# A two-block fp32 model in one kernel: the embeddings' projection in rounded parts, and low parts placed elsewhere on VectorE

## The chip, the cores and the metric

The kernel runs on one core of one Trainium2 chip. The metric is the device time in microseconds (us) of one execution, taken as the median of several runs. PE is TensorE, DVE VectorE, ACT ScalarE, POOL GpSimd, SP SyncE.

## What is computed

256 tokens of width 1024 go through a first block of two layers and a second block of two layers. The change touches only the two layers of the first block. One of them, cut to what matters:

```python
for i in range(DEPTH):                                  # DEPTH = 2
    xn = rmsnorm(h, norm_g[i])
    proj = xn @ w_in[i]                                 # hf hq hi nq kv ... hgo hz nz
    o_hg = hgrn2_chunkwise(hq, log_f, k_hg, hi)         # the gated recurrence
    y_hg = rmsnorm(o_hg, hgrn_onorm_g[i]) * sigmoid(hgo) * silu(hz)
    o_nsa = gates[0] * o_cmp + gates[1] * o_slc + gates[2] * o_win    # three attentions
    y_nsa = o_nsa * silu(nz)
    h = h + concatenate([y_hg, y_nsa]) @ w_out[i]
    gate = sigmoid(rmsnorm(h, ple_norm_g[i]) @ w_pg[i]) # w_pg: 1024 x 1024
    h = h + gate * (p[i] @ w_pp[i])                     # p[i]: 256 x 256, w_pp: 256 x 1024
```

Everything is fp32. `p[i]` are the embeddings of layer i, and `p[i] @ w_pp[i]` is their projection.

## The kernel before

**Panels.** All weights come in panels of 1 MB (128 partitions by 2048 columns, fp32), in the fixed order of `panel_plan`. SP loads them (`load_panel`, DMA issued at line 2831) into one of three raw slots (`RAW`, "panels" in the profile). For nearly all of them ACT then makes a high part, rounded to fp32r (`high_part`, line 1393, "panels_high"), and DVE the low part, raw minus high (`low_part`, line 2026, "panels_low"), each again in three slots. A product of two fp32 matrices is then three fp32r matmuls into one PSUM bank: weights low by input high, weights high by input low, weights high by input high (`product3`, lines 479 to 481). Panels named in `AS_THEY_ARE` (the compression weights, the projection "pp", a small one in block two) have no parts; PE multiplies them as plain fp32 (`small_chunk`, line 497), and their raw slot is free only when PE is done with it.

**Order.** The order on PE is written out by hand. ACT and DVE follow lists that PE's code fills while it is built (`agenda`, `todo`); between steps they make the parts of the next panels wherever `split_high` and `split_low` are called, as far as slots are free by then. Each engine works strictly through its own list. PE waits for a panel by counting low parts (`split`, `pe.wait_ge(low_ready, SPLIT_NO[key] + 1)`), and low parts are made in panel order.

**The recurrence.** Its decay matrices are built in eight levels, each in two halves g = 0, 1. For each, PE multiplies key and query blocks (`level`, line 788), then DVE copies the result out (lines 2271, 2278 or 2282) and multiplies query and key by the forget gates (lines 2300 to 2302), which the next level on PE needs. PE runs the levels in pairs between panels: level 5 between the halves of the panels vv0 and vv1, then the sums of squares of the heads, level 6, a small product ("hid", line 850), the first half of gate panel hgo0 (`gate_chunk`, 24 matmuls at lines 479 to 481), level 7, the second half of hgo0, and so on through hgo1, hz0, hz1, nz0, nz1. DVE's steps there are level 5, "gates" (a low part call, then the attention gates, lines 2334 and 2335), level 6, "hidden" (a low part call, then four small instructions from line 2361), level 7, "k_norm".

**The embeddings.** At the start SP loads `p` of both layers into the tile of q_rope; PE transposes both (line 766, banks 3 and 4) after the panels hi of layer 0; ACT copies them to "p_transposed". Late in each layer, after the output panels wo0 to wo3, PE runs pp: 16 products of 128x128 by 128x256, eight for groups 0 and 1, then the sum of squares of the norm (`folded_sum`, lines 588 and 592), then eight for groups 2 and 3. Next come the panels pg0 to pg3 of the gate, whose input is the normed residual: ACT turns the sum into 1/rms (two instructions on rinv), and DVE and ACT in turn make each of the eight 128x256 chunks (`normed`, lines 1989, 1417, 1985). PE's first matmul on pg0 waits for the first chunk, the next products for the next.

Of the kernel before, what the change touches and what calls it, by code (L numbers as in the profile page):

```python
# [8 lines left out]
P = 128  # L9
T = 256  # L10
NT = T // P
D = 1024
ND = D // P
DEPTH = 2
# [98 lines left out]
ODD_PANELS += [(f"{name}{h}", "mix1_w_in_2", c0 + 256 * h, 256) for name, c0 in  # L113
               (("zg", 512), ("zu", 0), ("fv", 2048)) for h in range(2)]
ODD_PANELS += [(f"wo{g}", "mix1_w_out_2", 256 * g, 256) for g in range(4)]
AS_THEY_ARE = ("cmp0", "cmp1", "pp", "ff")
BY_ROWS = ("hi0", "hi1", "zg0", "zg1", "fv0", "fv1", "vv0", "vv1")
NKH = ND // 2

# [44 lines left out]
def build(nc, a, out):  # L164
# [4 lines left out]
    with ExitStack() as ctx:  # L169
# [5 lines left out]
        def sem(name):  # L175
            if name not in sems:
                sems[name] = ctx.enter_context(nc.semaphore(name))
            return sems[name]
# [111 lines left out]
            flevel[n] = FLV[:, at:at + w]  # L290
            at += w
        xt = FK[:, :].rearrange("p (n d) -> p n d", n=NT)
        ptok = QR[:, :].rearrange("p (l d) -> p l d", l=2 * NT)
        PTR = ctx.enter_context(nc.sbuf_tensor("p_transposed", [P, 1024], F32))
        ptr = PTR[:, :].rearrange("p (l k t) -> p l k t", l=DEPTH, k=2)
        vrows = v3(QN, 8)
        FINAL, OUT, TS = UK[:, :], KZ, SS[:, 0:8]

# [19 lines left out]
        def bank(name):  # L318
            return ps[fills[name][0]]
# [47 lines left out]
        rope_ready, k_rope_ready = sem("q_rope_terms_ready"), sem("k_rope_terms_ready")  # L367
        q_turned, k_turned = sem("q_sine_terms_added"), sem("k_sine_terms_added")
        kz_ready = sem("k_padded_ready")
        blocks_ready = sem("cmp_blocks_ready")  # L370
        gate_exp_ready, gates_ready = sem("gate_exp_ready"), sem("gates_ready")
        hid_exp_ready, hidden_ready = sem("cmp_hidden_exp_ready"), sem("cmp_hidden_ready")
# [48 lines left out]
        def _(pe):  # L421
            last_done = [None]

            def begin(name, b):

                k = bank_fills[b]
                bank_fills[b] += 1
                fills[name] = (b, k)
                if k > 0:
                    pe.wait_ge(psum_free[b], k)  # L430
                return ps[b]
# [315 lines left out]
            for l in range(DEPTH):  # L747
# [8 lines left out]
                        two_chunks(f"hq{g}_{l}", 3 + g, (f"hq{g}", l), normed=nidx if g == 0 else None)  # L756
                tokens([f"hi{n}_{l}" for n in range(NT)], 5, [(f"hi{h}", l) for h in range(2)], normed=l == 0)
                if l == 0:

                    pe.wait_ge(const_landed, 16)  # L760
                    pe.wait_ge(p_landed, 16)
                    for m in range(DEPTH):
                        begin(f"p{m}", 3 + m)
                        for k in range(2):
                            for n in range(NT):
                                ins = pe.transpose(ps[3 + m][:, k * T + n * P:k * T + (n + 1) * P],
                                                   ptok[:, m * NT + n, k * P:(k + 1) * P], ident)
                        done(f"p{m}", ins)

                def level(n, g):  # L770

# [263 lines left out]
                for ks in (range(0, 6), range(6, ND)):  # L1035
                    output_rows(3, ks)

                landed(("pp", l))
                for g in range(4):
                    b = (7, 6, 1, 2)[g]  # L1040
                    if g == 2:
                        folded_sum(nidx)
                    begin(f"pp{g}_{l}", b)
                    for j in range(2):
                        ins = small_chunk(ps[b][:, j * T:(j + 1) * T], raw_panel(("pp", l), 2, 1024),
                                          (2 * g + j) * P, ptr[:, l], nk=2)
                    done(f"pp{g}_{l}", ins)
                release(("pp", l))
                first_two([f"pg{g}_{l}" for g in range(2)], (4, 5), [(f"pg{g}", l) for g in range(2)], nidx)
# [319 lines left out]
        def _(act):  # L1369
# [187 lines left out]
            for l in range(DEPTH):  # L1557
# [18 lines left out]
                for n in range(NT):  # L1576
                    copy_out(f"hi{n}_{l}", vh[:, n, :], bank(f"hi{n}_{l}")[:, :])
                    split_after(f"hi{n}_{l}")
                if l == 0:
                    for m in range(DEPTH):  # L1580
                        copy_out(f"p{m}", PTR[:, m * 512:(m + 1) * 512], bank(f"p{m}")[:, :])
                log_exp()
                dest = {"nq0": QN[:, 0:512], "nq1": QN[:, 512:1024], "ct": PCT[:, :], "hgo0": SG[:, 0:512], "hgo1": SG[:, 512:1024],
                        "hz0": HZ[:, 0:512], "hz1": HZ[:, 512:1024], "nz0": NZ[:, 0:512], "nz1": NZ[:, 512:1024]}
# [108 lines left out]

                split_after(f"wo_{l}_0")
                squares(nidx, lambda g: drained(act, f"wo_{l}_{g}"), lambda g: split_after(f"wo_{l}_{max(g, 1)}") if g != 1 else None)

                def pp_out(g):
                    copy_out(f"pp{g}_{l}", PP[:, g * 512:(g + 1) * 512], bank(f"pp{g}_{l}")[:, :])
# [259 lines left out]
        def _(dve):  # L1958
# [281 lines left out]
            for l in range(DEPTH):  # L2240
# [63 lines left out]

                for g in range(2):
                    split_after(f"hq{g}_{l}")
                in_units = parts_out = False
                for place, kind, *arg in agenda[l]:
                    if kind == "level":
# [18 lines left out]
                        if l == 0:  # L2328
                            bf16_tables()
                    elif kind == "gates":  # L2330
                        split_low(place)
                        for n in range(NT):
                            drained(dve, f"vv{n}_{l}")
                        link(V.tensor_scalar(GT[:, :], GT[:, :], 1.0, None, ALU.add))
# [22 lines left out]
                    elif kind == "hidden":  # L2357
# [8 lines left out]
                        V.tensor_copy(HIDV[:, :].rearrange("p (g r c) -> p g r c", g=2, r=4),  # L2366
                                      HID[:, 32:64].rearrange("p (g c) -> p g c", g=2).unsqueeze(2)
                                      .to_broadcast([P, 2, 4, 16])).then_inc(hidden_ready, 1)
                    elif kind == "cmp_kv":
                        full(dve, f"vc_{l}")  # L2370
                        V.tensor_tensor(v3(VCB, 8), const("head16").unsqueeze(2).to_broadcast([P, 8, 64]),
# [81 lines left out]
                        split_low(place)  # L2453

                add_out(f"wo_{l}_", "", 2 * l + 1)
                normed(2 * l + 1, "ple_norm_g", 8 * l)
                if l == DEPTH - 1:
                    V.memset(PB[:, 0:1024], 0.0).then_inc(bd_zeroed, 1)
# [342 lines left out]
        def _(sp):  # L2801
# [42 lines left out]
            for tile, r, n, c0, c1, src in vec_dmas[1::2]:  # L2844
# [1 line left out]
            load_panel(3)  # L2846
            load_panel(4)
            sp.dma_start(CN[:, 2 * P:], a["const_table"][:, 2 * P:]).then_inc(const_landed, 16)
            sp.dma_start(ptok.rearrange("p (l n) d -> p l n d", l=DEPTH),
                         a["p"][:, 0].rearrange("l (n p) d -> p l n d", p=P)).then_inc(p_landed, 16)  # L2850
            sp.dma_start(LM[:, :], a["mask_table"]).then_inc(masks_landed, 16)
            sp.dma_start(BF[0:8, 0:1], a["fox_bf_2"].rearrange("a h -> h a")).then_inc(bias_landed, 16)

# [24 lines left out]
            for n, (key, *_) in enumerate(LOADS):  # L2878
                if n > SLOTS + 1 and (len(key) == 2 or key[0] != "down" and key[2] == 0):
                    load_panel(n)  # L2880
                name, l, *r = key
                if name == "cmp0":
                    if l > 0:
                        b, k = fills[f"vc_{l - 1}"]
                        sp.wait_ge(psum_full[b], k + 1)
                    for c0, kv in ((0, 0), (64, 0), (P, 1)):
                        sp.dma_start(W2[:, c0:c0 + 64], a["cmp_w2"][l, kv]).then_inc(w2_landed, 16)
                if name == "ga1":
                    sp.wait_ge(bd_zeroed, 1)
                    for at, w in ((0, "lru_wa_2"), (512, "lru_wx_2")):  # L2890
                        src = a[w][0].rearrange("(c r) i j -> r i c j", r=2)
                        for r in range(2):
                            dst = PB[64 * r:64 * r + 64, at:at + 512].rearrange("p (c m) -> p c m", c=4)
                            sp.dma_start(dst[:, :, 64 * r:64 * r + 64], src[r]).then_inc(bd_landed, 16)
                if name == "fk0":
                    sp.dma_start(FINAL, a["final_norm_2"].unsqueeze(0).to_broadcast([P, D])).then_inc(gain_landed, 16)
                    sp.dma_start(PT[:, 0:1024].rearrange("p (h s) -> p h s", h=8),
                                 a["sgu_w_2"][0].rearrange("h t s -> t h s")).then_inc(sgu_landed, 16)
                    for h in range(8):
                        r, c = h % 2, h // 2  # L2900
                        sp.dma_start(AC[64 * r:64 * r + 64, c * P:(c + 1) * P],
                                     a["sgu_b_2"][0, h:h + 1, :].to_broadcast([64, P])).then_inc(bt_landed, 16)
                if name == "value" and r == [0]:
                    ffn(l)
# [27 lines left out]
```

## Time and profile before

| What | Value |
|---|---|
| median of 3 runs | 971.55 us (971.46 to 971.69) |
| the profiled execution | 971.99 us, its span 970.0 us |
| PE busy | 953.6 us, 98% of the span, 7618 matmuls |
| DVE busy | 754.3 us, 78% |
| ACT busy | 615.6 us, 63% |
| mean granted TensorE clock | 0.999 of full |
| DMA | 164.33 MB, 169 GB/s |

The profile is of one execution, and its span runs from the first to the last instruction. A matmul's length in the timeline is that of its passage through the array; matmuls overlap, so what one costs is read from the distance between two starts. Plain fp32 products stand in the timeline as two records each. A time in brackets is idle time of that engine just before the row, with what ended it.

### The profile page before, as it was taken

The numbers are of one execution on the slowest core, as the hardware profiler recorded it, in microseconds if no ns is written. First come the engines' busy times: TensorE is split into PE (matmuls) and PEld (weight loads), VectorE is DVE, ScalarE is ACT, GpSimd is POOL, SyncE is SP. The second block draws the span as 40 slices with busy tenths as digits, with TensorE's granted clock in tenths as the row PEclk, the third lists the DMA queues.
The fourth block names the chain that finished last, engine by engine and source line by source line (L and its number), as shares of the span: only waits on it lengthen the run. The fifth ranks groups of instructions, "written<-read, shape, count | busy, mean of one in ns | idle before, by whom it ended". The sixth has DMA issues, their size and how long they took to land.

```text
span 970.0 us, 18775 instructions
## 1 busy us (share of the span) xinstructions
PE 953.6 (98%) x7618; PEld 875.2 (90%) x7618; DVE 754.3 (78%) x1132; ACT 615.6 (63%) x914; POOL 19.7 (2%) x33
## 2 busy tenths in 40 slices
PE   6999999999999999999999999999999999999997
PEld 6998989999989889999999999999998988888886
DVE  7967876797678777998788877778878598777685
ACT  5744885676447856787477556557657566555554
POOL 2000200000002000000000000000000000000000
PEclk9999999999999999999999999999999999999999
DMA  9666422465664233745546656557283446655541
GB/s 304 197 181 219 139 88 87 137 214 183 173 218 139 66 110 115 244 156 188 179 133 215 218 175 200 187 174 222 93 271 110 141 135 219 203 181 176 191 152 44
DMA packets 143869, 164.33 MB, mean 169 GB/s; under 512 B 6686, under 2 KB 130216, under 8 KB 143800
## 3 DMA queue, kind: packets, MB, share of 16 engines
q1 hardware_dynamic: 142408, 161.90, 51.9%
q0 software_dynamic: 928, 0.52, 0.4%
q8 instruction: 51, 0.84, 0.4%
q10 hardware_dynamic: 464, 0.93, 0.3%
q14 instruction: 18, 0.15, 0.0%
HBM read 161.89 MB, written 1.05 MB: 168 GB/s over the span
## 4 chain that ended last, share of the span: by engine, by line
PE 87%; DVE 5%; ACT 4%; DMA 2%; issue 1%; SPq 0%; DVEq 0%; ACTq 0%
PE ps L479 19%; PE ps L480 18%; PE ps L481 18%; PE ps L1259 14%; PE ps L1257 7%; DMA panels<-in_w_in 2%; DVE panels_low L2026 2%; ACT panels_high L1393 2%; PE ps L497 1%; PE ps L692 1%; PE ps L717 1%; PE ps L788 1%; PE ps L1299 1%; DVE squares L1989 1%; PE ps L703 1%
## 5 line engine op out<-in xcount | busy, mean ns | idle before, releaser
L2026 DVE TENSOR_TENSOR panels_low<-panels,panels_high 128x2048 fp32r<-128x2048 f32 (+1 forms) x145 | 327.5, 2261 | 63.2 <-ACT panels_high L1393 62.6
L1393 ACT CAST panels_high<-panels 128x2048 fp32r<-128x2048 f32 (+1 forms) x145 | 273.4, 1887 | 85.7 <-PE ps L481 63.2
L479 PE MATMUL ps<-input_parts,panels_low 128*128 128x256 f32 x832 | 240.2, 289 | 0.2 <-DVE panels_low L2026 0.2
L480 PE MATMUL ps<-input_parts,panels_high 128*128 128x256 f32 x832 | 235.2, 283 | 0.0
L481 PE MATMUL ps<-input_parts,panels_high 128*128 128x256 f32 x832 | 235.1, 283 | 0.0
L1259 PE MATMUL ps<-input_parts,panels_high 128*128 128x512 f32 x608 | 214.0, 396 | 0.0
L1257 PE MATMUL ps<-input_parts,panels_low 128*128 128x256 f32 x608 | 170.6, 281 | 0.7 <-DVE panels_low L2026 0.7
L479 PEld LDWEIGHTS ps<-input_parts,panels_low 128*128 128x128 f32 x832 | 159.2, 191 | 2.4 <-issue 1.7
L480 PEld LDWEIGHTS ps<-input_parts,panels_high 128*128 128x128 f32 x832 | 159.3, 191 | 0.7 <-issue 0.5
L481 PEld LDWEIGHTS ps<-input_parts,panels_high 128*128 128x128 f32 x832 | 159.3, 191 | 0.0
L1259 PEld LDWEIGHTS ps<-input_parts,panels_high 128*128 128x128 f32 x608 | 114.1, 188 | 26.4
L1257 PEld LDWEIGHTS ps<-input_parts,panels_low 128*128 128x128 f32 x608 | 114.7, 189 | 2.5 <-issue 1.3
L479 PE MATMUL ps<-ffn_hidden_high,panels_low 128*128 128x256 f32 x320 | 91.2, 285 | 1.1 <-DVE panels_low L2026 1.0
L481 PE MATMUL ps<-ffn_hidden_high,panels_high 128*128 128x256 f32 x320 | 90.4, 283 | 0.0
L480 PE MATMUL ps<-ffn_hidden_low,panels_high 128*128 128x256 f32 x288 | 81.2, 282 | 0.0
L479 PEld LDWEIGHTS ps<-ffn_hidden_high,panels_low 128*128 128x128 f32 x320 | 60.8, 190 | 2.1 <-DVE panels_low L2026 1.2
L481 PEld LDWEIGHTS ps<-ffn_hidden_high,panels_high 128*128 128x128 f32 x320 | 60.2, 188 | 0.0
L480 PEld LDWEIGHTS ps<-ffn_hidden_low,panels_high 128*128 128x128 f32 x288 | 54.2, 188 | 0.3
L1923 ACT CAST ffn_hidden_high<-values_hg 128x512 fp32r<-128x512 f32 x22 | 13.7, 621 | 57.1 <-DVE values_hg L2707 53.7
L1892 ACT COPY forget_key<-ps 128x512 f32<-128x512 f32 x36 | 21.0, 583 | 44.5 <-PE ps L1259 44.5
L479 PE MATMUL ps<-unscaled,panels_low 128*128 128x256 f32 x160 | 46.2, 289 | 0.0
L481 PE MATMUL ps<-unscaled,panels_high 128*128 128x256 f32 x160 | 45.2, 283 | 0.0
(342 smaller groups left out, 1626.6 us busy)
## 6 DMA issues: line engine op xcount, KB each, us to landing
panels<-in_ffn_up SPq DMA_DIRECT2D x44, 1024.0 KB, 5.0
panels<-in_w_in SPq DMA_DIRECT2D x29, 1024.0 KB, 5.8
panels<-in_ffn_down SPq DMA_DIRECT2D x22, 1024.0 KB, 4.9
panels<-in_mix_w_in SPq DMA_DIRECT2D x20, 1024.0 KB, 5.7
panels<-in_w_out SPq DMA_DIRECT2D x8, 1024.0 KB, 5.3
panels<-in_w_pg SPq DMA_DIRECT2D x8, 1024.0 KB, 5.1
panels<-in_mix_w_out SPq DMA_DIRECT2D x8, 1024.0 KB, 5.2
panels<-in_w_in SPq DMA_DIRECT2D x6, 512.0 KB, 5.7
```

The source lines that it names most:

```text
L479: pe.matmul(dst, w[1], x[0], start=start, stop=False if not kw else True, **kw)
L480: pe.matmul(dst, w[0], x[1], start=False, stop=False if not kw else True, **kw)
L481: return pe.matmul(dst, w[0], x[0], start=False, stop=stop, **kw)
L497: ins = pe.matmul(dst, w3[:, k, col:col + m], x3[:, k, :], start=(k == 0), stop=(k == nk - 1))
L692: ins = pe.matmul(ps[b + r][:, 0:2 * w].rearrange("p (k s) -> p k s", k=2), q[h, n * P:(n + 1) * P], keys[h, :, r, 0:w], start=False, stop ...
L703: pe.transpose(ps[6][:, r * T:r * T + P], probs[bb][0][:, r, :], ident)
L1257: pe.matmul(both[:, 0, :], w_low, xh3[:, k, :], start=(k == 0), stop=True, skip_group_check=True)
L1259: ins = pe.matmul(both, w_high, x_parts[:, :, k, :], start=False, stop=True, skip_group_check=True)
L1393: nc.scalar.copy(high_slots[slot][:, 0:size], raw[n % SLOTS][:, 0:size]).then_inc(high_ready, 1)
L1892: nc.scalar.copy(sums[par][:, s, :], up_halves[half][:, :, 0, :]).then_inc(half_out, 1)
L1923: nc.scalar.copy(gh3[par], hidden[par]).then_inc(gh_ready, 1)
L2026: V.tensor_tensor(low_slots[slot][:, 0:size], raw[n % SLOTS][:, 0:size], high_slots[slot][:, 0:size].bitcast(F32), ALU.subtract).then_inc( ...
```

## The change

The panel pp is no longer taken as it is: it gets a high and a low part like the others, and its products become three fp32r matmuls each (`product3`). With that, each later panel stands one place further in the count of parts and in the three slots. The transposed embeddings get two parts as well: ACT rounds the transposed PSUM bank to a high part, DVE subtracts it for the low part, ahead of recurrence level 0. The tile has room for one layer, so the transposes are made once in each layer, and `p` of layer 1 is loaded after pg0 of layer 0. In the norm after the output panels, ACT and DVE make the parts of one more panel, pg1, after those of pg0 (`split_after(f"wo_{l}_3")`). In DVE's step "gates" the call for low parts is gone; "hidden" keeps its call at its start and gets a second one at its end.

```diff
-AS_THEY_ARE = ("cmp0", "cmp1", "pp", "ff")
+AS_THEY_ARE = ("cmp0", "cmp1", "ff")
...
-        ptok = QR[:, :].rearrange("p (l d) -> p l d", l=2 * NT)
-        PTR = ctx.enter_context(nc.sbuf_tensor("p_transposed", [P, 1024], F32))
-        ptr = PTR[:, :].rearrange("p (l k t) -> p l k t", l=DEPTH, k=2)
+        ptok = v3(QR, 4)[:, 0:NT, :]
+        PTR = ctx.enter_context(nc.sbuf_tensor("p_transposed_parts", [P, 1024], F32R))
+        p_parts = PTR[:, :].rearrange("p (s k t) -> p s k t", s=2, k=2)
...
                 if l == 0:
-
                     pe.wait_ge(const_landed, 16)
-                    pe.wait_ge(p_landed, 16)
-                    for m in range(DEPTH):
-                        begin(f"p{m}", 3 + m)
-                        for k in range(2):
-                            for n in range(NT):
-                                ins = pe.transpose(ps[3 + m][:, k * T + n * P:k * T + (n + 1) * P],
-                                                   ptok[:, m * NT + n, k * P:(k + 1) * P], ident)
-                        done(f"p{m}", ins)
+                pe.wait_ge(p_landed, 16 * (l + 1))
+                begin(f"p{l}", 3)
+                for k in range(2):
+                    for n in range(NT):
+                        ins = pe.transpose(ps[3][:, k * T + n * P:k * T + (n + 1) * P], ptok[:, n, k * P:(k + 1) * P],
+                                           ident)
+                done(f"p{l}", ins)
...
-                landed(("pp", l))
+                split(("pp", l))
+                drained(pe, f"p{l}")
+                w = parts(("pp", l), 2, 1024)
...
-                        ins = small_chunk(ps[b][:, j * T:(j + 1) * T], raw_panel(("pp", l), 2, 1024),
-                                          (2 * g + j) * P, ptr[:, l], nk=2)
+                        c = (2 * g + j) * P
+                        for k in range(2):
+                            ins = product3(ps[b][:, j * T:(j + 1) * T], [t[:, k, c:c + P] for t in w],
+                                           (p_parts[:, 0, k, :], p_parts[:, 1, k, :]), k == 0, k == 1)
...
@@ ACT @@
-                if l == 0:
-                    for m in range(DEPTH):
-                        copy_out(f"p{m}", PTR[:, m * 512:(m + 1) * 512], bank(f"p{m}")[:, :])
+                full(act, f"p{l}")
+                nc.scalar.copy(PTR[:, 0:512], bank(f"p{l}")[:, :]).then_inc(ph_ready, 1)
...
                 squares(nidx, lambda g: drained(act, f"wo_{l}_{g}"), lambda g: split_after(f"wo_{l}_{max(g, 1)}") if g != 1 else None)
+                split_after(f"wo_{l}_3")
...
@@ DVE, ahead of the agenda's levels @@
+                dve.wait_ge(ph_ready, l + 1)
+                V.tensor_tensor(PTR[:, 512:1024], bank(f"p{l}")[:, :], PTR[:, 0:512].bitcast(F32),
+                                ALU.subtract).then_inc(free(f"p{l}"), 1)
...
                     elif kind == "gates":
-                        split_low(place)
                         for n in range(NT):
                             drained(dve, f"vv{n}_{l}")
...
                     elif kind == "hidden":
                         split_low(place, SPLIT_NO[("hgo1", l)] + 1)
...
+                        split_low(place, SPLIT_NO[("hgo1", l)] + 1)
...
                 add_out(f"wo_{l}_", "", 2 * l + 1)
+                split_after(f"wo_{l}_3")
                 normed(2 * l + 1, "ple_norm_g", 8 * l)
...
@@ SP @@
-            sp.dma_start(ptok.rearrange("p (l n) d -> p l n d", l=DEPTH),
-                         a["p"][:, 0].rearrange("l (n p) d -> p l n d", p=P)).then_inc(p_landed, 16)
+            psrc = a["p"][:, 0].rearrange("l (n p) d -> l p n d", p=P)
+            sp.dma_start(ptok, psrc[0]).then_inc(p_landed, 16)
...
+                if (name, l) == ("pg0", 0):
+                    b, k = fills["n0D1_3"]
+                    sp.wait_ge(psum_full[b], k + 1)
+                    sp.dma_start(ptok, psrc[1]).then_inc(p_landed, 16)
```

**Where instructions move.** First place: DVE in each layer of the first block, at the steps "gates", level 6 and "hidden". "panels_low" is the low part of a panel, here of hgo0 and hgo1 (x2); "nsa_gates" is the step "gates"; "decay_diag", "gate_o", "query", "forget_key" are level 6, half 0 then half 1; "small" opens the step "hidden". Before:

```order
L2026 TENSOR_TENSOR panels_low<-panels,panels_high 128x2048 [waits panel_high_ready] x2
L2334 TENSOR_SCALAR nsa_gates<-nsa_gates 128x48 [waits psum_free6,psum_free5]
L2335 RECIPROCAL nsa_gates<-nsa_gates 128x48 [waits vector_step]
L2278 COPY decay_diag<-ps 32x4x32 [waits psum_full7]
...
L2300 TENSOR_TENSOR gate_o<-gate_o 128x8 [waits vector_step,hg_level_ready]
L2301 TENSOR_TENSOR query<-query,gate_o 128x8x32
L2302 TENSOR_TENSOR forget_key<-forget_key,gate_o 128x8x32
L2278 COPY decay_diag<-ps 32x4x32 [waits psum_full0]
...
L2361 TENSOR_SCALAR small<-small 128x64 [waits cmp_hidden_exp_ready]
```

And in the changed kernel:

```order
L2339 TENSOR_SCALAR nsa_gates<-nsa_gates 128x48 [waits psum_free6,psum_free5]
L2340 RECIPROCAL nsa_gates<-nsa_gates 128x48 [waits vector_step]
L2281 COPY decay_diag<-ps 32x4x32 [waits psum_full7]
...
L2303 TENSOR_TENSOR gate_o<-gate_o 128x8 [waits vector_step,hg_level_ready]
L2304 TENSOR_TENSOR query<-query,gate_o 128x8x32
L2305 TENSOR_TENSOR forget_key<-forget_key,gate_o 128x8x32
L2281 COPY decay_diag<-ps 32x4x32 [waits psum_full0]
...
L2029 TENSOR_TENSOR panels_low<-panels,panels_high 128x2048 [waits panel_high_ready] x2
L2366 TENSOR_SCALAR small<-small 128x64 [waits cmp_hidden_exp_ready]
```

Both low parts moved from ahead of the gates and level 6 to behind both halves of level 6.

Second place: PE at the same point, the same in both kernels. The first two rows are level 6 (halves 0 and 1), the third is "hid", the fourth the first matmul on gate panel hgo0:

```order
L788 MATMUL ps<-query,forget_key 32x32 [waits psum_free7,hg_level_ready]
...
L788 MATMUL ps<-query,forget_key 32x32 [waits psum_free0,hg_level_ready]
...
L850 MATMUL ps<-consts,nsa_z 128x32 [waits psum_free3]
...
L479 MATMUL ps<-input_parts,panels_low 128x256 [waits panel_low_ready,psum_free6]
...
L788 MATMUL ps<-query,forget_key 64x64 [waits psum_free7,hg_level_ready]
```

Nothing moved here: the matmul on hgo0 waits for a low part and stands ahead of level 7 (the last row, half 0).

Third place: ACT at the norm after the output panels. "squares" is the square of a quarter of the residual, "rinv" the 1/rms, "panels_high" the high part of a panel. In the changed kernel:

```order
L1396 CAST panels_high<-panels 128x2048 [waits psum_full3,panel_landed1]
L1382 ACTIVATE squares<-residual 128x512 [waits psum_free5]
L1396 CAST panels_high<-panels 128x2048 [waits psum_full5,panel_landed2]
L1382 ACTIVATE rinv<-ps,eps 128x256 [waits psum_full0]
L1382 ACTIVATE rinv<-rinv 128x256 [waits psum_free0]
L1420 CAST input_parts<-squares 128x256 [waits normed_f32_ready] x8
```

The second cast, of pg1, is new here; before, the square is followed by rinv at once. On DVE a second low part stands likewise between the last sum of the residual and the first instruction of `normed`.

## Rows read from the trace of the kernel before

**Rows 1.** The page: busy time, engines of the last chain, cast to high parts.

```profile
PE 953.6 (98%) x7618; PEld 875.2 (90%) x7618; DVE 754.3 (78%) x1132; ACT 615.6 (63%) x914; POOL 19.7 (2%) x33
...
PE 87%; DVE 5%; ACT 4%; DMA 2%; issue 1%; SPq 0%; DVEq 0%; ACTq 0%
...
L1393 ACT CAST panels_high<-panels 128x2048 fp32r<-128x2048 f32 (+1 forms) x145 | 273.4, 1887 | 85.7 <-PE ps L481 63.2
```

**Rows 2.** Waits of PE, whole span: total, times, longest us.

```profile
PE ps L788 <- DVE forget_key L2302: 1.5, 2, 0.8
```

**Rows 3.** Timeline of PE, layer 0: start us, length us, engine, line, operation.

```profile
87.17 0.70 PE L788 MATMUL ps<-query,forget_key 128*32 128x32 f32 x32
...
88.26 0.36 PE L479 MATMUL ps<-input_parts,panels_low 128*128 128x256 f32 x1
...
92.79 0.68 PE L788 MATMUL ps<-query,forget_key 128*64 128x64 f32 x8 [0.80 <-DVE forget_key L2302]
```

**Rows 4.** Timeline of DVE there; in brackets the idle time before, and its releaser.

```profile
84.23 2.29 DVE L2026 TENSOR_TENSOR panels_low<-panels,panels_high 128x2048 fp32r<-128x2048 f32 x1 [1.12 <-ACT panels_high L1393]
87.07 2.29 DVE L2026 TENSOR_TENSOR panels_low<-panels,panels_high 128x2048 fp32r<-128x2048 f32 x1 [0.55 <-ACT panels_high L1393]
...
89.87 0.52 DVE L2278 COPY decay_diag<-ps 32x128 f32<-32x128 f32 x2
...
92.32 0.42 DVE L2302 TENSOR_TENSOR forget_key<-forget_key,gate_o 128x256 f32<-128x256 f32 x1
```

**Rows 5.** Timeline of PE at the embeddings' projection, layer 0.

```profile
177.80 3.62 PE L497 MATMUL ps<-p_transposed,panels 128*128 128x256 f32 x16
181.25 0.59 PE L588 MATMUL ps<-squares,consts 128*128 128x256 f32 x2
...
182.55 3.62 PE L497 MATMUL ps<-p_transposed,panels 128*128 128x256 f32 x16
...
186.12 0.28 PE L480 MATMUL ps<-input_parts,panels_high 128*128 128x256 f32 x1
186.24 0.28 PE L481 MATMUL ps<-input_parts,panels_high 128*128 128x256 f32 x1
```

**Rows 6.** Timeline of ACT and DVE at the norm beside it.

```profile
182.75 0.47 ACT L1379 ACTIVATE rinv<-ps,eps 128x256 f32<-128x256 f32 x1 [3.17 <-PE ps L592]
...
183.71 0.88 DVE L1989 SCALAR_TENSOR_TENSOR squares<-residual,vectors,rinv 128x256 f32<-128x256 f32 x2 [2.45 <-ACT rinv L1379]
184.66 0.43 DVE L1985 TENSOR_TENSOR input_parts<-squares,input_parts 128x256 fp32r<-128x256 f32 x1
```

**Rows 7.** Timeline of ACT and DVE at the first recurrence level.

```profile
49.78 1.08 ACT L1384 COPY p_transposed<-ps 128x512 f32<-128x512 f32 x2
...
49.99 0.69 DVE L2288 TENSOR_TENSOR query<-query,forget_key 128x512 f32<-128x512 f32 x1
...
55.42 0.30 DVE L2271 COPY_PREDICATED decay_blocks<-level_masks,ps 128x128 f32<-128x128 int32 x1 [2.54 <-PE ps L788]
```

**Rows 8.** Windows at the end; the third number from the right is the clock.

```profile
964.00:965.00 1.00, 0.26 (x2) 0.00 (x0) 0.32 (x1) 0.69 (x2) 0.00 (x0) 1.00 0.00 0
...
966.00:967.00 1.00, 0.00 (x0) 0.00 (x0) 1.00 (x2) 0.00 (x0) 0.00 (x0) 1.00 0.59 246
967.00:968.00 1.00, 0.00 (x0) 0.00 (x0) 0.19 (x1) 0.00 (x0) 0.00 (x0) 0.71 0.98 387
968.00:969.00 1.00, 0.00 (x0) 0.00 (x0) 0.00 (x0) 0.00 (x0) 0.00 (x0) 0.50 1.00 385
```

**Rows 9.** Timeline of PE's first microseconds.

```profile
8.96 1.97 PE L611 MATMUL ps<-consts,forget_key 128*128 128x128 f32 x8 [1.15 <-DMA forget_key<-in_x]
...
11.15 0.41 PE L481 MATMUL ps<-ffn_hidden_high,panels_high 128*128 128x256 f32 x1
11.37 0.41 PE L479 MATMUL ps<-ffn_hidden_high,panels_low 128*128 128x256 f32 x1
...
11.75 0.28 PE L481 MATMUL ps<-ffn_hidden_high,panels_high 128*128 128x256 f32 x1
```

More of the change, by code:

```diff
@@ L369, in build @@
         kz_ready = sem("k_padded_ready")
+        ph_ready = sem("p_transposed_high_ready")
         blocks_ready = sem("cmp_blocks_ready")
```

## Prediction

> **What bounds the kernel now.** The page comes first. PE is busy for 98% of the span and holds 87% of the chain that ended last, DVE is at 78% and ACT at 63% [rows 1]. So work that is taken from PE, or a wait put on it, moves the end by about its own length; work on DVE and ACT counts only where PE waits for it. Second, the list of PE's waits. Most belong to the start; of those inside the layers the largest is for the recurrence: 1.5 us, twice, 0.8 us at most [rows 2]. It is level 7, half 1, once in each layer, and layer 1 repeats layer 0 at this place to within 0.1 us. Third, the timelines around the two places that are edited.
>
> A difference of 0.2% (1.9 us) is about what a measurement can tell here from no change. The sum below is a difference, made in the profiled execution of 971.99 us (span 970.0 us, and 2.0 us around it); it is added to the median of 971.55 us, which lies 0.4 us under that execution.
>
> **The low parts moved behind level 6.** Before, DVE makes the low part of hgo0 from 84.23 us and that of hgo1 from 87.07 us, 2.29 us each, and starts level 6 late, at 89.87 us; its last instruction starts at 92.32 us and ends at 92.74 us. Level 7, half 1, starts on PE 0.05 us after that, at 92.79 us, with 0.80 us of idle time ahead [rows 3, 4]. Moving the low parts away frees this chain, which is worth the 1.5 us in the two layers.
>
> But PE wants hgo0 before level 7. Its first matmul on that panel starts at 88.26 us [rows 3], 1.7 us after the low part is there (84.23 + 2.29 = 86.52). In the changed kernel the low part is behind both halves of level 6 in DVE's own list, and DVE cannot pass them. Level 6 is first on PE: it starts at 87.17 us and half 0, half of 0.70 us, is done at 87.52 us [rows 3]. DVE then needs 92.74 - 89.87 = 2.87 us for both halves [rows 4]. So:
> - DVE starts level 6 at 87.52 + 0.05 = 87.57 us and ends it at 90.44 us;
> - the low part of hgo0 takes 2.29 us, to 92.73 us;
> - PE starts on hgo0 at about 92.8 us in place of 88.26 us: 4.5 us later.
>
> What else is queued there: behind PE's wait stands everything, since PE runs in its own order. On DVE the low part of hgo1 ends 2.3 us later, at 95.0 us, which PE wants only a panel half, level 7 and another half after 92.8 us, so not before 99 us. Then "hidden" and level 7 follow, some 2.5 us later than before, while PE itself is 4.5 us later: no second wait. The loads of the panels that reuse these raw slots go out up to 6 us later, for casts that stand behind PE by more than that.
>
> Net in each layer: 4.5 us new wait, less the wait on level 7. For both: 2 x 4.5 - 1.5 = **+7.5 us**. The bounds: were DVE faster by its pipelining (level 6 in 2.4 us, the distance of its first and last start, 92.32 - 89.87) it is 4.0 us each, +6.5; were the hand-overs 0.15 us each instead of 0.05, +7.9.
>
> **The projection in rounded parts.** Before, 32 records of plain fp32 a layer: 16 between 177.80 and 181.25 us, 3.45 us, then the norm's sum, then 16 more from 182.55 us; the matmuls at the fp32r pace go on from 186.12 - 0.12 = 186.00 us, again 3.45 us [rows 5]. Together 6.9 us. After: 48 fp32r matmuls at the distance of 186.24 - 186.12 = 0.12 us [rows 5], 5.76 us. That is 1.15 us less on PE in each layer.
>
> Not all of it arrives, since pg0 waits for the norm. The sum now ends 0.6 us earlier, and ACT, idle for 3.17 us before 182.75 us, could answer at 182.2 us. But DVE has a new low part (pg1) in the 2.45 us that it was idle before 183.71 us [rows 6]: the cast of pg1 can start on ACT at 182.75 - 3.17 = 179.58 us, takes 1.89 us [rows 1], so DVE works on it from 181.5 to 183.8 us. The norm's first instruction on DVE then starts at 183.8 us, where it stood before, 0.1 us later in fact. Its first chunk was ready at 184.66 + 0.43 = 185.09 us [rows 6] and is ready at 185.2 us now, against PE's 184.85 us. So PE resumes at 185.25 us in place of 186.00 us: 0.75 us gained per layer, and I take it that the later chunks come as fast as PE uses them (six matmuls each, 0.72 us). For both layers **-1.5 us**, within -2.3 us (the norm holds nothing up) and -0.6 us (cast or low part of pg1 half a microsecond late). A rule of the Trainium skill speaks for more: "FP8 and Floating Point Precision", section "TensorE Precision Notes", has true fp32 as four passes through the array. By it, three products instead of four passes would save a quarter, 1.7 us a layer instead of 1.15 us; the trace shows 6.9 against 5.76 us and decides.
>
> **The embeddings' parts.** PE makes the same eight transposes, four of them in each layer: nothing in sum. Casts and low parts are added: DVE gets 0.69 us (a 128x512 instruction) ahead of level 0, and must wait for ACT's one copy, which ended at 49.78 + 0.54 = 50.3 us. Level 0's four instructions, which ended at 50.68 us, then end at about 53 us, and the low part of the next panel at 55.3 us. DVE was idle for 2.54 us before level 1 at 55.42 us, so this just fits [rows 7]. I cost it at nothing; if its cover were gone, it would be 0.5 us in a layer. The load of `p` of layer 1 moves 256 KB beside panels of 1 MB; SP's added wait is for scores that PE finishes before wo3 is split, which the next panel load waits for anyway. Nothing.
>
> **The clock.** This is the unknown. PE has no wait of 4.5 us inside the layers now. At the end of the run it stops at 964.26 us; the granted clock is still 1.00 in the window from 966 us, 0.71 in the next, 0.50 (1.2 GHz) from 968 us [rows 8]. It fell about 3.1 us after the last matmul. A wait of 4.5 us is longer than that. At the start, matmuls begin again at 8.96 us, are 0.22 us apart at 11.15 us and of full-speed length from 11.75 us [rows 9]: 2.8 us of slow work, of which 1 - 0.12/0.22, some 1.25 us, are lost. So each wait costs between 0 (the clock holds) and 1.25 us. One instance of a fall does not say that it always comes so soon; I take one fall in two waits, **+1.2 us**, and keep 0 and +2.5.
>
> **Sum.** 7.5 - 1.5 + 1.2 = +7.2 us, so 971.55 + 7.2 = **978.7 us**, slower by 0.7%.
>
> **The rivals.**
> - The clock holds in both waits: 7.5 - 1.5 = +6.0, 977.5 us. For it: one example of a fall, at the end of the run, is thin. Chance 0.28.
> - It falls in both: 7.5 - 1.5 + 2.5 = +8.5, 980.0 us. For it: the wait is longer than the 3.1 us of rows 8 each time. Chance 0.27. The Trainium skill sides with it: "TensorE: Matmul & The Clock Gate", section "HAM oscillation — how this bites in real kernels", says that idle gaps between bursts of matmuls put the engine back to half its clock, and each gap pays anew.
> - **Faster**: the low part of hgo0 does arrive before PE wants it, and only hgo1's stands behind level 6. The high part is there at 84.2 us, where DVE stood idle for it [rows 4], so there is room for 2.29 us before 88.26 us. Then level 7 waits no more (-1.5), the projection gives -1.5 to -2.3: -3.4, 968.1 us. The point that decides is whether the low part ends by 88.26 us. Against it stands the order of the changed kernel, where both low parts follow level 6. Chance 0.04.
> - **No change**: PE's delay is taken up further on, because another engine sets the end after all. It would need waits of PE behind the layers that shrink by 6 us; with PE busy for 98% of the span [rows 1] and no wait over 0.8 us in the layers there is next to nothing to give back. 971.5 us, chance 0.04.
>
> My forecast, one fall in two, has 0.37.
>
> **Range and chances.** 975.8 to 981.2 us: it spans the three clock cases, with 1 to 1.5 us for a new wait of 4.0 instead of 4.5 us and a projection worth 0.6 to 2.3 us. All three are slower by over 0.2%: 0.92. Within 0.2%: 0.04. Faster: 0.04.
>
> **What will show it.** In the changed kernel's trace PE has a wait for "panels_low" of over 4 us in each layer, right behind level 6 and "hid", released by the low part of hgo0; the wait for forget_key at level 7 is gone; DVE is idle ahead of level 6 and has both low parts behind it. Matmuls on p_transposed_parts stand 0.12 us apart, and pg0 starts up to 0.2 us after them with DVE as releaser. In the windows behind the new waits the granted clock is 1.00 or lower, which decides among the three cases. I am wrong if PE goes from "hid" to hgo0 without a gap, or if such a gap is under 3 us.

## The result, and the profile after

The changed kernel takes 982.24 us (median of 4 runs, 981.97 to 982.35) against 971.60 us before (971.46 to 971.69): +10.6 us, a ratio of 1.0108 [1.0096, 1.0120]. The forecast was 978.7 us and its range ended at 981.2 us. The sign and the place were right, the size was not. Two lines of the page of the profiled execution, and its span:

```profile
span 980.3 us, 18849 instructions
PE 956.4 (98%) x7650; PEld 879.5 (90%) x7650; DVE 759.9 (78%) x1136; ACT 618.7 (63%) x916; POOL 19.7 (2%) x33
PE 85%; DVE 6%; ACT 5%; issue 2%; DMA 1%; SPq 0%; DVEq 0%; ACTq 0%
```

Beside [rows 1], PE's share of the chain has fallen by 2 points; DVE, ACT and "issue" have each gained one, and DMA has lost one. PE is still busy for 98% of the span. But its busy time *rose* by 2.8 us, though 2.3 us of matmul work was taken out of the projection. At a lower clock PE is busy for longer with the same work (matmuls 0.21 us apart instead of 0.12, below), so a busy time that rises where work was removed is the first sign of the clock. The list of PE's waits:

```profile
PE ps L480 <- DVE panels_low L2029: 9.9, 5, 4.5
PE ps L604 <- DMA q_nope<-in_norm_g: 6.3, 1, 6.3
PE ps L1260 <- DVE panels_low L2029: 0.8, 2, 0.4
PE ps L480 <- DVE input_parts L1988: 0.5, 2, 0.2
```

The wait for forget_key of [rows 2] is gone. In its place stands one for panels_low: 9.9 us in five waits, the longest 4.5 us. The third row belongs to both kernels, and so does a wait of some 6 us at the start (5.7 us before, 6.3 us here). DVE's timeline in layer 0 shows why:

```profile
87.15 0.58 DVE L2281 COPY decay_diag<-ps 32x128 f32<-32x128 f32 x2 [1.71 <-PE ps L787]
...
89.66 0.42 DVE L2305 TENSOR_TENSOR forget_key<-forget_key,gate_o 128x256 f32<-128x256 f32 x1
90.00 4.49 DVE L2029 TENSOR_TENSOR panels_low<-panels,panels_high 128x2048 fp32r<-128x2048 f32 x2
```

Level 6 starts on DVE at 87.15 us, 2.7 us earlier than in [rows 4], and takes 2.85 us to the start of the two low parts. The 4.49 us are both of them, shown as one row; hgo0's is the first half, done by 92.3 us. PE's timeline there, and the same row in layer 1:

```profile
86.66 0.70 PE L787 MATMUL ps<-query,forget_key 128*32 128x32 f32 x32
87.29 0.63 PE L849 MATMUL ps<-consts,nsa_z 128*128 128x32 f32 x4
92.43 0.55 PE L480 MATMUL ps<-input_parts,panels_low 128*128 128x256 f32 x1 [4.51 <-DVE panels_low L2029]
92.78 0.42 PE L481 MATMUL ps<-input_parts,panels_high 128*128 128x256 f32 x1
92.99 0.42 PE L482 MATMUL ps<-input_parts,panels_high 128*128 128x256 f32 x1
...
97.77 1.14 PE L787 MATMUL ps<-query,forget_key 128*64 128x64 f32 x16
...
293.74 0.55 PE L480 MATMUL ps<-input_parts,panels_low 128*128 128x256 f32 x1 [4.51 <-DVE panels_low L2029]
```

The last row is the one of layer 1. Two things are to be seen. PE is idle for 4.51 us in front of hgo0, once in each layer. And behind it the matmuls are not 0.12 us apart but 0.21 us (92.78 to 92.99): the 24 of this panel half take 5.34 us, from 92.43 to level 7 at 97.77 us. The windows across that place (PEclk is the third number from the right):

```profile
88.00:90.00 2.00, 0.00 (x0) 0.00 (x0) 1.93 (x8) 2.00 (x3) 0.00 (x0) 1.00 0.00 0
90.00:91.00 1.00, 0.00 (x0) 0.00 (x0) 1.00 (x2) 0.97 (x2) 0.00 (x0) 0.91 0.00 0
91.00:97.00 6.00, 4.57 (x21) 4.60 (x22) 4.60 (x6) 2.43 (x4) 0.00 (x0) 0.50 0.61 194
97.00:98.00 1.00, 1.00 (x9) 0.83 (x8) 0.00 (x0) 0.00 (x0) 0.00 (x0) 0.68 1.09 350
...
292.00:293.00 1.00, 0.00 (x0) 0.00 (x0) 1.00 (x1) 1.00 (x3) 0.00 (x0) 0.60 0.00 0
293.00:299.00 6.00, 5.26 (x24) 5.19 (x24) 3.90 (x6) 1.74 (x3) 0.00 (x0) 0.50 0.72 232
299.00:300.00 1.00, 1.00 (x16) 0.89 (x16) 0.17 (x1) 0.00 (x0) 0.00 (x0) 0.98 1.11 350
```

The granted clock falls to its lower level (0.50, 1.2 GHz) within the wait, in both layers, and stays there for nearly the whole panel half. A row that holds both levels gives the moment: 0.91 in the row from 90 us puts the fall at 90.8 us, 0.60 in the one from 292 us at 292.2 us, 2.9 and 3.0 us after PE's last matmul; the rise is at 97.6 and 299.0 us. The Trainium skill, "TensorE: Matmul & The Clock Gate", section "HAM oscillation — how this bites in real kernels", describes this course: each gap between bursts pays for a slow start anew. The trace agrees on that. The section counts 1.67 us of throttled time per gap, in a kernel whose bursts of 16 matmuls are about 2 us long; here the burst goes on, and the rows show 5.3 us of slow work.

Where the time went, from the starts of the same instructions in both traces: PE is 0.5 us ahead of the kernel before at level 6 of layer 0 (four of the eight transposes now stand in layer 1). Past level 7 it is 5.45 us behind, past the projection 4.67, past layer 1's transposes 5.11, past layer 1's level 7 11.19, and past its projection 10.42 us behind, which stays to the end. So the moved low parts cost 6.0 and 6.1 us, the projection gives 0.8 us twice, and the transposes give 0.5 us and take 0.4.

### The profile page after: what moved, and what is told of

Same layout as the page of the kernel before. It is cut to its first block, busy times and chain, and to the rows that moved or that the text cites. A ratio compares the mean times of both kernels' runs of the same rounds, so it can differ in the third digit from the quotient of the medians.

```text
span 980.3 us, 18849 instructions
## 1 busy us (share of the span) xinstructions
PE 956.4 (98%) x7650; PEld 879.5 (90%) x7650; DVE 759.9 (78%) x1136; ACT 618.7 (63%) x916; POOL 19.7 (2%) x33
## 4 chain that ended last, share of the span: by engine, by line
PE 85%; DVE 6%; ACT 5%; issue 2%; DMA 1%; SPq 0%; DVEq 0%; ACTq 0%
PE ps L480 19%; PE ps L481 18%; PE ps L482 18%; PE ps L1262 14%; PE ps L1260 7%; ACT panels_high L1396 2%; DVE panels_low L2029 2%; PE ps L693 1%; PE ps L787 1%; PE ps L718 1%; DMA panels<-in_w_in 1%; PE ps L598 1%; DVE squares L1992 1%; PE ps L1302 1%; DVE input_parts L1988 1%
## 5 line engine op out<-in xcount | busy, mean ns | idle before, releaser
L2029 DVE TENSOR_TENSOR panels_low<-panels,panels_high 128x2048 fp32r<-128x2048 f32 (+1 forms) x147 | 332.0, 2262 | 59.1 <-ACT panels_high L1396 58.5
L1396 ACT CAST panels_high<-panels 128x2048 fp32r<-128x2048 f32 (+1 forms) x147 | 277.1, 1886 | 85.2 <-PE ps L482 63.9
L481 PE MATMUL ps<-input_parts,panels_high 128*128 128x256 f32 x832 | 237.7, 286 | 0.0
L482 PE MATMUL ps<-input_parts,panels_high 128*128 128x256 f32 x832 | 237.6, 286 | 0.0
L481 PEld LDWEIGHTS ps<-input_parts,panels_high 128*128 128x128 f32 x832 | 161.6, 194 | 0.6 <-issue 0.5
L482 PEld LDWEIGHTS ps<-input_parts,panels_high 128*128 128x128 f32 x832 | 161.6, 194 | 0.0
L1262 PEld LDWEIGHTS ps<-input_parts,panels_high 128*128 128x128 f32 x608 | 114.3, 188 | 26.1
```

The source lines that it names most:

```text
L481: pe.matmul(dst, w[0], x[1], start=False, stop=False if not kw else True, **kw)
L482: return pe.matmul(dst, w[0], x[0], start=False, stop=stop, **kw)
L1262: ins = pe.matmul(both, w_high, x_parts[:, :, k, :], start=False, stop=True, skip_group_check=True)
L1396: nc.scalar.copy(high_slots[slot][:, 0:size], raw[n % SLOTS][:, 0:size]).then_inc(high_ready, 1)
L2029: V.tensor_tensor(low_slots[slot][:, 0:size], raw[n % SLOTS][:, 0:size], high_slots[slot][:, 0:size].bitcast(F32), ALU.subtract).then_inc( ...
```

## The experiments

All were compared with the kernel before on the same chip: 971.53 us for the first four, 971.86 us for the last four.

**e1: the low parts back ahead of the gates.** The rest of the change stays.

```diff
                     elif kind == "gates":
+                        split_low(place)
                         for n in range(NT):
```

> The changed kernel with the call for low parts put back at its old place in DVE's step gates, so that both low parts (hgo0, hgo1) stand ahead of level 6 again; everything of the projection stays. Theory (all of the loss comes from the moved low parts and the clock after them): 971.6 - 1.6 = 970.0 us, the 0.8 and 0.7 us waits at level 7 back, no wait of PE over 1 us after the start, granted clock 1.00 throughout the layers. Rival (the projection's added casts, low parts and slots cost the part of the loss that I had not counted, some 3.5 us): 974 to 975 us.

Measured 969.89 us (969.66 to 970.17), ratio 0.9983 [0.9973, 0.9992], mean clock 0.999; level 7 waits for forget_key again (1.4 us in two). The projection and the embeddings' parts without the moved low parts give 1.6 us, as the sum had it (1.5).

**e2: the move alone**, made in the kernel before.

```diff
                     elif kind == "gates":
-                        split_low(place)
                         for n in range(NT):
```

> The kernel before with the call for low parts taken out of the step gates and nothing else changed. Theory: two waits of 4.5 us on the low part of hgo0, each followed by some 5 us at half clock, minus the waits at level 7: 971.6 + 12.0 = 983.6 us, the granted clock 0.50 for about 7 us in each of the two layers. Rival (the projection carries 3.5 us of the loss): 979 to 980 us.

Measured 983.13 us (981.86 to 983.98), ratio 1.0114 [1.0097, 1.0131]. Its waits of PE:

```profile
PE ps L479 <- DVE panels_low L2026: 9.7, 5, 4.5
```

With e1 this places the loss in the call that is gone: 983.13 - 971.53 = +11.6 us for it and -1.6 us for the rest make +10.0 us, beside the +10.6 us of both together; the 0.6 us between them are within the spread of e2's runs (2.1 us).

**e3: PE kept busy through the wait.** 36 more matmuls ahead of the one on hgo0, on data that are there, into a bank that the real products then overwrite; they are no part of the reference's computation.

```diff
                         begin(f"{name}{g}_{l}", b)
+                        if key[0] == "hgo0":
+                            for i in range(36):
+                                pe.matmul(ps[b][:, 0:T], xh3[:, i % ND, 0:P], xh3[:, i % ND, :], start=True,
+                                          stop=True, skip_group_check=True)
                         split(key)
```

> The changed kernel with 36 more fp32r matmuls of 128x256 (4.3 us at 0.12 us apart) on PE ahead of its wait for hgo0; their result is overwritten by the first matmul on hgo0. Theory (the clock falls because PE stands still): the wait is filled, the granted clock stays 1.00, PE resumes when the low part is there, as before, and the work after it is at full speed: 982.2 - 2 x 2.35 = 977.5 us. Rival (the slow stretch behind the wait has another cause, such as DMA traffic or operands that come late): no change, 982.2 us.

Measured 977.23 us (976.99 to 977.70), ratio 1.0058 [1.0042, 1.0075]. The timeline, then windows over the place:

```profile
87.80 4.55 PE L805 MATMUL ps<-input_parts 128*128 128x256 f32 x36
92.38 0.39 PE L480 MATMUL ps<-input_parts,panels_low 128*128 128x256 f32 x1
...
95.45 1.15 PE L787 MATMUL ps<-query,forget_key 128*64 128x64 f32 x16
```

```profile
90.00:92.00 2.00, 2.00 (x19) 2.00 (x18) 2.00 (x2) 1.97 (x5) 0.00 (x0) 1.00 0.00 0
92.00:94.00 2.00, 1.97 (x16) 1.77 (x16) 2.00 (x2) 1.49 (x2) 0.00 (x0) 1.00 0.19 35
94.00:97.00 3.00, 3.00 (x33) 2.80 (x32) 2.47 (x8) 0.00 (x0) 0.00 (x0) 1.00 1.05 360
```

The first real matmul starts at 92.38 us, in the changed kernel at 92.43: the wait is as long, it is only filled. But the panel half now takes 3.07 us (92.38 to 95.45) instead of 5.34, and the kernel is 5.0 us faster for 72 added matmuls. So the clock alone costs 2.27 us at this place and 5.0 us in all (4.7 us between the two profiled spans, 980.3 and 975.6 us), and the delay of the low part makes the rest: 977.23 us is the forecast's case "the clock holds", 977.5 us. DMA traffic as the cause of the slow stretch is ruled out with it: the loads still run (360 GB/s from 94 us), and the clock stays at 1.00.

**e4: only hgo0's low part back ahead of the gates.**

```diff
                     elif kind == "gates":
+                        split_low(place, SPLIT_NO[("hgo0", l)] + 1)
                         for n in range(NT):
```

> The changed kernel with only the low part of hgo0 put back ahead of level 6; that of hgo1 stays behind it. Theory: hgo0 is there 1.7 us before PE wants it, level 6 is done early enough for level 7 (its 1.5 us in two layers go), and hgo1's low part ends near 92.8 us, 4 us before PE wants it: 971.6 - 1.5 - 1.6 = 968.5 us. Rival (level 7 or hgo1 becomes late in its place): 970.0 us or more, with a wait of PE on panels_low or forget_key there.

Measured 967.86 us (967.69 to 968.28), ratio 0.9961 [0.9947, 0.9975]. DVE's timeline:

```profile
82.88 2.28 DVE L2029 TENSOR_TENSOR panels_low<-panels,panels_high 128x2048 fp32r<-128x2048 f32 x1
...
90.34 2.29 DVE L2029 TENSOR_TENSOR panels_low<-panels,panels_high 128x2048 fp32r<-128x2048 f32 x1
```

and PE's waits on the two releasers in question (none is on forget_key):

```profile
PE ps L1260 <- DVE panels_low L2029: 0.7, 2, 0.4
PE ps L480 <- DVE input_parts L1988: 0.5, 2, 0.2
PE ps L480 <- DVE panels_low L2029: 0.4, 2, 0.2
```

One low part ahead of level 6 and one behind it meets both of PE's needs. This is the place and the price of the forecast's "faster" rival (968.1 us), which the change itself did not make.

**e5: the same in the kernel before**, to see whether the parts add up.

```diff
                     elif kind == "gates":
-                        split_low(place)
+                        split_low(place, SPLIT_NO[("hgo0", l)] + 1)
                         for n in range(NT):
```

> The kernel before with hgo0's low part left ahead of level 6 and only hgo1's moved behind it; the projection stays plain fp32. Theory (the two parts of the change add up): the waits at level 7 go, 971.5 - 1.5 = 970.0 us, so that e4 (967.9) is this plus the projection's 1.6 to 2.0 us. Rival (e4's gain needs both parts together, since the projection shifts the panels' slots): no change, 971.5 us.

Measured 969.84 us (969.67 to 970.03), ratio 0.9979 [0.9969, 0.9988]. With e1: -2.0 - 1.6 = -3.6 us, and e4 has -3.7. The two parts add up. The gain of 2.0 us is more than the 1.5 us of level 7's waits: its two halves take 1.07 us of PE's time without the wait (97.77 to 98.84 us in the changed kernel) and took 2.09 us with it (91.31 to 93.40 us in the kernel before), 1.0 us less in each layer.

**e6: half as many matmuls in the wait**, 18 instead of 36, so that PE is idle for 2.2 us.

```diff
-                            for i in range(36):
+                            for i in range(18):
```

> As e3_pe_kept_busy, with 18 matmuls (2.2 us) in place of 36, at the start of the wait, so that PE still stands still for 2.4 us. Theory (the clock falls some 3 us after PE's last matmul, as at 90.9 and 292.6 us in the changed kernel's windows): the clock holds, 977.3 us as with 36. Rival (any wait of 2 us or more in place of work brings it down): between 980 and 982 us, granted clock 0.50 behind the wait.

Measured 979.85 us (978.63 to 980.71), ratio 1.0078 [1.0062, 1.0093]: a miss for the expectation that such a short wait leaves the clock alone. The timeline, then the windows:

```profile
87.82 2.38 PE L805 MATMUL ps<-input_parts 128*128 128x256 f32 x18
92.40 0.58 PE L480 MATMUL ps<-input_parts,panels_low 128*128 128x256 f32 x1 [2.20 <-DVE panels_low L2033]
...
96.92 1.15 PE L787 MATMUL ps<-query,forget_key 128*64 128x64 f32 x16
```

```profile
91.00:92.00 1.00, 0.00 (x0) 0.00 (x0) 1.00 (x1) 1.00 (x3) 0.00 (x0) 1.00 0.00 0
92.00:93.00 1.00, 0.60 (x2) 0.60 (x3) 1.00 (x2) 0.97 (x2) 0.00 (x0) 0.67 0.00 0
93.00:95.00 2.00, 2.00 (x11) 2.00 (x11) 1.97 (x3) 0.53 (x1) 0.00 (x0) 0.50 0.69 191
95.00:96.00 1.00, 1.00 (x8) 1.00 (x7) 0.69 (x3) 0.00 (x0) 0.00 (x0) 0.63 1.09 383
96.00:98.00 2.00, 2.00 (x26) 1.80 (x24) 0.37 (x2) 0.00 (x0) 0.00 (x0) 1.00 1.10 362
...
292.00:293.00 1.00, 0.16 (x1) 0.17 (x2) 1.00 (x2) 0.97 (x3) 0.00 (x0) 1.00 0.00 0
293.00:294.00 1.00, 1.00 (x8) 1.00 (x9) 1.00 (x1) 0.96 (x1) 0.00 (x0) 0.86 0.14 16
```

The clock fell here too: in layer 0 at 92.3 us (0.67 in the window from 92 us), just before PE took up work again, and in layer 1 at 293.7 us (0.86 in the window from 293 us), 0.9 us *after* PE had taken it up at 292.84 us. The slow stretch was shorter, from 92.3 to 95.7 us in layer 0: the panel half took 4.52 us, 1.45 us more than in e3, and 4.56 us in layer 1. So the fall does not come at the same point of the wait even within one execution; the four runs lie 2.1 us apart, those of e3 0.7 us. (The 292.6 us in the expectation is 292.2 us by the window.)

**e7: e1 with pg1's parts behind the norm**, as they were before, to price the early parts.

```diff
                 squares(nidx, lambda g: drained(act, f"wo_{l}_{g}"), lambda g: split_after(f"wo_{l}_{max(g, 1)}") if g != 1 else None)
-                split_after(f"wo_{l}_3")
...
                 add_out(f"wo_{l}_", "", 2 * l + 1)
-                split_after(f"wo_{l}_3")
                 normed(2 * l + 1, "ple_norm_g", 8 * l)
```

> e1_calls_back with the parts of pg1 made behind the norm (the calls after wo_3 taken out on ACT and DVE). Theory: the norm starts 0.6 us earlier, but pg1's high part is cast at 191.4 us only, its low part ends near 195.8 us, and PE, which wants it at 190.6 us, waits some 5 us in each layer with the clock falling behind it: 969.9 + 2 x (5.2 - 0.4 + 2.3) = 984 us. Rival (pg1's early parts are what holds the norm up, and are not needed so early): 969 us.

Measured 982.61 us (981.73 to 983.56), ratio 1.0106 [1.0091, 1.0121].

```profile
182.93 0.88 DVE L1991 SCALAR_TENSOR_TENSOR squares<-residual,vectors,rinv 128x256 f32<-128x256 f32 x2 [1.82 <-ACT rinv L1382]
...
192.71 2.28 DVE L2028 TENSOR_TENSOR panels_low<-panels,panels_high 128x2048 fp32r<-128x2048 f32 x1
```

```profile
195.14 0.56 PE L480 MATMUL ps<-input_parts,panels_low 128*128 128x256 f32 x1 [4.63 <-DVE panels_low L2028]
```

Here the same thing happens at another place: DVE is idle ahead of the norm, the low part of pg1 comes behind it, and PE stands for 4.63 us (4.50 in layer 1) and then works at half clock (0.50 from 194 to 200 us, the matmuls 0.21 us apart again). 982.61 - 969.89 = 12.7 us, for two waits of 9.1 us in sum: 1.8 us a wait above its length. That is net of what the later parts give: the norm's first instruction no longer stands behind pg1's low part (182.93 us against 183.06 in e1), and e1's waits of 0.5 us for input_parts are gone.

**e8: the casts of e4 one step earlier on ACT**, for a better version.

```diff
-                squares(nidx, lambda g: drained(act, f"wo_{l}_{g}"), lambda g: split_after(f"wo_{l}_{max(g, 1)}") if g != 1 else None)
-                split_after(f"wo_{l}_3")
+                squares(nidx, lambda g: drained(act, f"wo_{l}_{g}"), lambda g: split_after(f"wo_{l}_{g + 1}"))
```

> e4_one_ahead with ACT's casts of pg0 and pg1 one square earlier each (pg0 after the square of quarter 1, pg1 after that of quarter 2, ahead of the last square). Theory: pg1's high part is there 1.7 us earlier, DVE makes its low part right behind pg0's, from 181.2 to 183.5 us, and the norm starts 0.2 to 0.3 us earlier in each layer: 967.3 us. Rival (the last square, now behind a cast that waits for wo3 on PE, holds up the norm's sum): 968 to 969 us.

Measured 967.31 us (967.22 to 967.43), ratio 0.9951 [0.9938, 0.9965]. DVE's timeline:

```profile
177.54 4.49 DVE L2028 TENSOR_TENSOR panels_low<-panels,panels_high 128x2048 fp32r<-128x2048 f32 x2
181.94 0.88 DVE L1991 SCALAR_TENSOR_TENSOR squares<-residual,vectors,rinv 128x256 f32<-128x256 f32 x2
```

The gap of 0.16 us between the two low parts is closed, the norm follows at once, and the wait for input_parts has left PE's list. This is the fastest version: 4.5 us under the kernel before, 14.9 us under the changed one.

## Why the prediction was right and wrong

- **The low parts behind level 6: right.** Forecast a wait of 4.5 us on hgo0 in each layer, released by its low part; measured 4.51 and 4.51 us. Level 7's wait of 0.8 us went, as forecast. No second wait followed. Inside the term two small errors point opposite ways: from "hid" to hgo0 PE loses 4.67 us (92.43 - 87.29 against 88.26 - 87.79), not 4.5, and level 7 gives back 1.0 us a layer, not 0.75. e3, where only the wait's length is left, came to 977.23 us where this part and the projection gave 977.5 us.
- **The projection: right.** Forecast -0.75 us a layer, measured -0.78 and -0.77 us. What limits it is what the sum had: the norm behind the low part of pg1. The rows:

```profile
184.41 2.29 DVE L2029 TENSOR_TENSOR panels_low<-panels,panels_high 128x2048 fp32r<-128x2048 f32 x1
186.86 2.29 DVE L2029 TENSOR_TENSOR panels_low<-panels,panels_high 128x2048 fp32r<-128x2048 f32 x1 [0.16 <-ACT panels_high L1396]
189.07 0.88 DVE L1992 SCALAR_TENSOR_TENSOR squares<-residual,vectors,rinv 128x256 f32<-128x256 f32 x2
...
190.59 0.36 PE L480 MATMUL ps<-input_parts,panels_low 128*128 128x256 f32 x1 [0.23 <-DVE input_parts L1988]
```

  The rinv that the norm needs was ready on ACT at 188.50 us (start 188.08, 0.42 us long), 0.6 us before DVE was free.
- **The embeddings' parts at nothing: right.** DVE's level 1 starts at 54.93 us, 0.49 us ahead of [rows 7] like the rest of that stretch. The slack was used up almost entirely:

```profile
50.34 0.69 DVE L2311 TENSOR_TENSOR p_transposed_parts<-ps,p_transposed_parts 128x512 fp32r<-128x512 f32 x1 [1.33 <-ACT p_transposed_parts L1583]
...
52.54 2.29 DVE L2029 TENSOR_TENSOR panels_low<-panels,panels_high 128x2048 fp32r<-128x2048 f32 x1
54.93 0.30 DVE L2274 COPY_PREDICATED decay_blocks<-level_masks,ps 128x128 f32<-128x128 int32 x1
```

- **The clock: the step that failed.** It was named as the unknown, its mechanism was right, and it was mis-sized twice. First the count: "one fall in two waits" was a halving for want of evidence; the clock fell in both, and so it did in e2 and e7 in their waits of 4.5 and 4.6 us. Second the price of one fall, put at 0 to 1.25 us: here the slow work was 5.34 us and the loss 5.34 - 3.07 = 2.27 us. The term was 2 x 2.3 = +4.6 us in place of +1.2; with it the sum is 7.5 - 1.5 + 4.6 = +10.6 us. That this meets the measured +10.6 to the tenth is luck: the profiled spans differ by 10.3 us, and e1 and e2 add up to +10.0.
- **Where the 1.25 us went wrong.** The price was read from the start of the run, and only from its second batch of matmuls, at 8.96 us [rows 9]. The first batch ran slowly as well; the same number of records of 128x128 later in the program takes about half as long:

```profile
5.85 1.97 PE L611 MATMUL ps<-consts,forget_key 128*128 128x128 f32 x8
...
47.30 1.03 PE L766 MATMUL ps<-consts,q_rope 128*128 128x128 f32 x8
```

  The slow work at the start was thus 2.0 us from 5.85 us and 2.8 us from 8.96 us, 4.8 us with 1.15 us of idle time between. By the prediction's own rule (1 - 0.12/0.22 of it is lost) that is an estimate of 2.2 us for a fall, close to the 2.27 us measured. The windows at that place give 1.00 for the granted clock while the matmuls stand 0.22 us apart, so there the pace has to be read from the distances. Whether the start and a wait must cost alike is not shown: e6 lost 1.45 us.
- **The range** reached to two falls at 1.25 us each plus about 1 us. Even the rival with two falls, 980.0 us, lies 2.2 us under the measured time, nearly all of it the price of a fall (2 x 1.0 us). At 2.2 us a fall that rival would have been 971.55 + 7.5 - 1.5 + 4.4 = 982.0 us.

## What to carry to other kernels

Before work is moved behind something on an in-order engine, list every consumer of that work and when each wants it: here the first low part was wanted 1.7 us after it was made and the second 7.4 us after (its first matmul stood at 96.74 us, its low part was there at 89.36), so moving one gives 2.0 us and moving both costs 11.6. A wait that a change puts on a busy TensorE can cost its length and then the work behind it at half clock: here 4.5 us of waiting cost 6.8. Price such a wait with a run that fills it with matmuls whose results nobody reads. Where the start of the program is all there is to go by, count its slow work from the very first matmul and set the upper bound above it.

## What was not expected of the hardware

- After a wait of 4.5 us, 5.3 us of steady matmul work ran slowly, in both layers of the changed kernel, in e2 and in e7. The start of the program, counted from its first matmul, has 4.8 us of it.
- The clock also fell after an idle time of 2.2 us (e6), once just before PE resumed and once 0.9 us after. The last matmul of the program before [rows 8] and the changed kernel's waits had suggested that it holds for some 3 us; e6 takes that away on one side, and the end of the changed kernel's run on the other: PE stops there at 974.5 us, and the clock falls at 978.3 us, 3.8 us later (1.00 in the window from 977 us, 0.64 in the one from 978 us). What decides when it falls, and how long it stays low, is open; the length of the one wait alone does not give it.
- 72 matmuls whose results nobody reads made a kernel 5.0 us faster. The better cure is to have no wait there: e8 is 9.9 us faster than that.
